# Powers on POOL instead of DVE, one more group of a in seven-product form, tiles due one group sooner

## The reference, cut to what matters

```python
proj = rmsnorm(x) @ w_in                      # v, bg, cg, za, u, zb, ga, gb
ya = (bg * causal_conv3(cg * v)) * silu(za) @ w_out_a
yb = gelu(s5_scan(u, ...))                    # complex diagonal recurrence, 64 groups of 64 states
yb = (yb * sigmoid(yb @ w_glu + b_glu)) * silu(zb) @ w_out_b
x1 = rmsnorm(x + (sigmoid(ga)*ya + sigmoid(gb)*yb) @ w_o)
# second block: modulation by cond @ w_ada, spatial gating, 16 heads of forgetting attention, w_out_2
```

## Time and profile before

| | |
|---|---|
| median of 3 runs | 2487.74 us (2487.32 to 2489.63) |
| the profiled execution, its own time | 2489.72 us |
| its span, first to last instruction | 2488.5 us |
| PE busy | 2465.3 us, 99% |
| DVE busy | 1737.4 us, 70% |
| ACT / POOL busy | 925.6 us / 411.5 us |
| granted PE clock, mean | 0.998 |

### The profile page before, as it was taken

The page is one execution under the profiler, slowest core; times in us unless marked ns, Lnnn a source line. Parts: engine busy times, 40 slices in busy tenths (PEclk is TensorE's granted clock), DMA queues, the critical chain, the costliest instruction groups (busy, mean ns, idle before and its releaser), DMA issues.

```text
span 2488.5 us, 32838 instructions
## 1 busy us (share of the span) xinstructions
PE 2465.3 (99%) x13084; PEld 2170.0 (87%) x13084; DVE 1737.4 (70%) x2313; ACT 925.6 (37%) x1267; POOL 411.5 (17%) x334
## 2 busy tenths in 40 slices
PE   9999999999999999999999999999999999999998
PEld 8888887888888899999888888878888888888888
DVE  7889999998998865666756666567565564467534
ACT  5323222222222245445422223333565564224432
POOL 0035554553543011211000000000000000000001
PEclk9999999999999999999999999999999999999999
DMA  5344444443333288988676777524322222556333
GB/s 203 105 125 145 141 134 129 138 133 110 122 113 109 98 205 200 201 204 182 225 255 217 228 242 231 170 87 152 102 85 77 85 85 86 195 178 210 119 127 127
DMA packets 124888, 378.43 MB, mean 152 GB/s; under 512 B 16192, under 2 KB 19520, under 8 KB 124736
## 3 DMA queue, kind: packets, MB, share of 16 engines
q1 hardware_dynamic: 115520, 342.77, 42.0%
q0 software_dynamic: 9216, 33.56, 7.6%
HBM read 346.84 MB, written 23.07 MB: 149 GB/s over the span
## 4 chain that ended last, share of the span: by engine, by line
PE 48%; DVE 2%; DMA 1%; ACT 0%; issue 0%; DVEq 0%; ACTq 0%; SPq 0%
PE bank L696 13%; PE bank L697 13%; PE bank L698 13%; PE bank L965 2%; PE bank L966 2%; PE bank L964 2%; PE bank L1018 1%; DMA SI<-scr_zb 1%; PE bank L1008 1%; PE bank L928 1%; DVE ACC L1583 0%; PE bank L1001 0%; PE bank L999 0%; DVE WL L1567 0%; PE bank L1060 0%
## 5 line engine op out<-in xcount | busy, mean ns | idle before, releaser
L1567 DVE TENSOR_TENSOR WL<-W,WH 128x1024 fp32r<-128x1024 f32 (+1 forms) x447 | 592.8, 1329 | 385.5 <-ACT WH L1136 384.6
L1136 ACT ACTIVATE WH<-W 128x1024 fp32r<-128x1024 f32 (+1 forms) x447 | 468.8, 1051 | 791.1 <-PE bank L698 475.0
L696 PE MATMUL bank<-hH,WH 128*128 128x512 f32 x1280 | 487.6, 381 | 1.5 <-DVE hL L1861 1.1
L698 PE MATMUL bank<-hH,WL 128*128 128x512 f32 x1280 | 485.9, 380 | 0.0
L697 PE MATMUL bank<-hL,WH 128*128 128x512 f32 x1280 | 485.9, 380 | 0.0
L696 PEld LDWEIGHTS bank<-hH,WH 128*128 128x128 f32 x1280 | 242.5, 189 | 44.9 <-issue 7.3
L698 PEld LDWEIGHTS bank<-hH,WL 128*128 128x128 f32 x1280 | 242.4, 189 | 34.3
L697 PEld LDWEIGHTS bank<-hL,WH 128*128 128x128 f32 x1280 | 242.7, 190 | 33.7
L696 PE MATMUL bank<-h2H,WH 128*128 128x512 f32 x624 | 239.8, 384 | 0.1
L698 PE MATMUL bank<-h2H,WL 128*128 128x512 f32 x624 | 236.6, 379 | 0.0
L697 PE MATMUL bank<-h2L,WH 128*128 128x512 f32 x624 | 236.6, 379 | 0.0
(11 more groups left out here) (365 smaller groups left out, 4898.7 us busy)
## 6 DMA issues: line engine op xcount, KB each, us to landing
W<-in_w SPq DMA_DIRECT2D x292, 512.0 KB, 3.5
W<-in_ada SPq DMA_DIRECT2D x96, 512.0 KB, 4.2
W<-in_w POOLq DMA_DIRECT2D x35, 512.0 KB, 6.0
W<-in_wa SPq DMA_DIRECT2D x32, 512.0 KB, 4.2
W<-in_wo SPq DMA_DIRECT2D x32, 512.0 KB, 3.6
W<-in_wvv SPq DMA_DIRECT2D x32, 512.0 KB, 4.2
WX<-in_w POOLq DMA_DIRECT2D x29, 512.0 KB, 6.3
WX<-in_w SPq DMA_DIRECT2D x24, 512.0 KB, 4.2
```

The lines of the kernel that those rows point to most:

```text
L696: e.matmul(o, wh, xh, start=first, stop=False)
L698: return e.matmul(o, wl, xh, start=False, stop=last)
L1136: e.activation(chunk_parts(n)[0][:, c], raw_chunk(n)[:, c], ACT.Copy).then_inc(sem["hi"], 1)
L1567: e.tensor_tensor(wl[:, c], raw_chunk(n)[:, c], wh[:, c].bitcast(F32), ALU.subtract).then_inc(sem["lo_v"], 1)
```

## The change

Four edits in one:

1. The powers leave DVE. DVE's generator keeps nine empty steps in their place; POOL gets a function `powers()` with the same operations, each waiting for the one before (`prm_p`). POOL calls it as soon as DVE has finished CB (`prm_v`), and before its first `stack_low`.
2. `PARAM_STEPS` is spread: step 10 falls at unit 18 (before: 19), steps 11 and 12 at units 19 and 20, and step 21 at unit 29 (before: 26). The tiles begin at unit 31 (29), take equal shares on all units, and end with group 5 of a (6).
3. `ST_C` goes from 8 to 7: group 7 of a is made as a seven-product pair.
4. The first two projections of wb are woven: pieces 0 to 6 of the first, 0 to 6 of the second, then piece 7 of both.

```diff
-PARAM_STEPS = [min(max(n - 4, 0), 9) + (3 * max(n - 18, 0) + 1) // 2 for n in range(27)]
-TILE_UNIT = 29
-TILE_SHARE = (5, 4)
-SSM_C = 6
-ST_C = 8
+PARAM_STEPS = [min(max(n - 4, 0), 9) + max(n - 17, 0) for n in range(30)]
+TILE_UNIT = 31
+TILE_SHARE = (1, 1)
+SSM_C = 5
+ST_C = 7
...
-        for d, p in enumerate(wb_p):
-            project(p, lambda k: BH[:, k, :], lambda k: BL[:, k, :], b_ready if d == 0 else None, (0,))
+        first = [unit(), None]
+        for i, ks in enumerate((range(7), range(7, 8))):
+            for d in range(2):
+                if (i, d) == (0, 1):
+                    first[1] = unit()
+                n, o = first[d], bank[bank_of[wb_p[d]]][:, :]
+                for k in ks:
...
+                    if d == 0:
+                        b_ready(k)
+                    c = slice(128 * k, 128 * k + 128)
+                    mm = triple(o, WH[:, n % NB, c], WL[:, n % NB, c], pairs(BH[:, k, :]), pairs(BL[:, k, :]),
+                                k == 0, k == 7)
+                if i == 1:
+                    mm.then_inc(sem["used"], 1)
+        for d, p in enumerate(wb_p[2:]):
+            project(p, lambda k: BH[:, k, :], lambda k: BL[:, k, :], None, (0,))
...
-            for big, levels in ((E0, 5), (W0, 4)):
+            for _ in range(9):
+                yield
...
+            def powers():
+                at = [0]
+                def step(ins):
+                    ins.then_inc(sem["prm_p"], 1)
+                    at[0] += 1
+                    e.wait_ge(sem["prm_p"], at[0])
+                e.wait_ge(sem["prm_v"], counts["param"])
+                step(e.tensor_copy(pr, cosz))
+                step(e.tensor_copy(pi, sinz))
+                for big, levels in ((E0, 5), (W0, 4)):
+                    step(e.memset(big[:, 0, :, 0:1], 1.0))
+                    step(e.memset(big[:, 1, :, 0:1], 0.0))
+                    for lv in range(levels):
+                        w = 1 << lv
...
+                        step(e.tensor_tensor(y1, a_r, b_r, ALU.mult))
+                        step(e.tensor_tensor(y2, a_i, b_i, ALU.mult))
+                        step(e.tensor_tensor(o_r, y1, y2, ALU.subtract))
+                        step(e.tensor_tensor(y1, a_r, b_i, ALU.mult))
+                        step(e.tensor_tensor(y2, a_i, b_r, ALU.mult))
+                        step(e.tensor_tensor(o_i, y1, y2, ALU.add))
+                        step(e.tensor_tensor(t1, pr, pr, ALU.mult))
+                        step(e.tensor_tensor(t2, pi, pi, ALU.mult))
+                        step(e.tensor_tensor(nr, pr, pi, ALU.mult))
+                        step(e.tensor_tensor(pr, t1, t2, ALU.subtract))
+                        step(e.tensor_scalar(pi, nr, 2.0, None, ALU.mult))
...
+            powers()
             stack_low(0)
             stack_low(1)
             for _ in range(4):
                 yield
-            e.wait_ge(sem["prm_v"], counts["param"])
             e.wait_ge(*nth("xl", 31))
             table(0, 0)
             table(0, 1)
```

More of the change, by code:

```diff
@@ L58 @@
     "sums": 1, "rms_v": 1, "rms_a": 1, "spread": 1, "rsa": 1, "u_rd": 1,
-    "prm": 16, "prm_v": 1, "cb0": 1, "ssm_v": 14, "ssm_p": 6, "ssm_a": 2, "ssm_lu": 1, "ssm_lb": 1,
+    "prm": 16, "prm_v": 1, "prm_p": 1, "cb0": 1, "ssm_v": 14, "ssm_p": 6, "ssm_a": 2, "ssm_lu": 1, "ssm_lb": 1,
     "ssm_bu": 1, "ssm_out": 1, "skip": 1,
@@ L458, in ssm_phases @@
         if n < TILE_UNIT:
-            return min(PARAM_PHASES, PARAM_STEPS[min(n, 26)])
+            return min(PARAM_PHASES, PARAM_STEPS[min(n, 29)])
         return PARAM_PHASES + 130 * tile_share(n) // tile_share(tiles_to)
@@ L898, in b_ready @@
             e.wait_ge(*nth("g_v", k))
-        for d, p in enumerate(wb_p):
-            project(p, lambda k: BH[:, k, :], lambda k: BL[:, k, :], b_ready if d == 0 else None, (0,))
+        first = [unit(), None]
[5 more added lines that the diff above has]
+                for k in ks:
+                    if k == 0:
+                        for w in bank_free[wb_p[d]]:
+                            e.wait_ge(*w)
+                    if d == 0:
[7 more added lines that the diff above has]
+            project(p, lambda k: BH[:, k, :], lambda k: BL[:, k, :], None, (0,))
         def a_ready(k):
@@ L2547, in stack_low @@
                 e.tensor_tensor(ul, URAW[0:32, j % 2, :], ul.bitcast(F32), ALU.subtract).then_inc(sem["ssm_lu"], 1)
+            def powers():
[4 more added lines that the diff above has]
+                    e.wait_ge(sem["prm_p"], at[0])
+                sinz, cosz, t1, t2 = (sm(i) for i in range(18, 22))
+                pr, pi, nr = (sm(i) for i in range(27, 30))
+                tmp, tmp2 = (T[:, i, :].rearrange("p (j n) -> p j n", n=16) for i in (2, 3))
+                e.wait_ge(sem["prm_v"], counts["param"])
[6 more added lines that the diff above has]
+                        w = 1 << lv
+                        a_r, a_i = big[:, 0, :, 0:w], big[:, 1, :, 0:w]
+                        o_r, o_i = big[:, 0, :, w:2 * w], big[:, 1, :, w:2 * w]
+                        b_r = pr.unsqueeze(2).to_broadcast([128, 32, w])
+                        b_i = pi.unsqueeze(2).to_broadcast([128, 32, w])
+                        y1, y2 = tmp[:, :, 0:w], tmp2[:, :, 0:w]
+                        step(e.tensor_tensor(y1, a_r, b_r, ALU.mult))
[9 more added lines that the diff above has]
+                        step(e.tensor_scalar(pi, nr, 2.0, None, ALU.mult))
             def table(j, part):
```

## The result

| | before | after |
|---|---|---|
| median, both measured in the same rounds | 2488.68 us | 2507.36 us |
| profiled execution's span | 2488.5 us | 2507.4 us |
| ratio after / before | | 1.0078, 95% interval 1.0064 to 1.0092 |

The change makes the kernel 18.7 us slower. The forecast was 2502.7 us, its range 2484 to 2516: 14 us over this median of the kernel before, 15 us over the one shown ahead of the prediction.

What follows compares the result with a forecast made beforehand. PE, busy for 99% of the span, was taken as the bound, with DVE setting the pace beside the rows. 2489.7 - 17.0 + 16.0 + 16 = 2504.7, less 2.0 to the median: 2502.7 us, range 2484 to 2516.

Steps and rivals of the forecast that it cites:

- The stand at `drive(0)`: PE at unit 29 waits for POOL's chain of powers and first low stack: 14.3 us plus slow clock, 16.0 us lost.
- Rival 3: POOL much later, each operation at its 1.79 ratio to DVE: 28.9 us lost before the first drive, 2515.6 us; chance 0.1.
- the tiles' start: Tile 0 starts some 20 us later than before, with its tables ready by then: costs nothing.
- Denser tiles beside a: One tile in 3.48 units overloads DVE beside a: 1.2 us a tile, 16 us lost, bounds nothing and 29 us.
- Readout waits gone beside the rows: Three PE waits at readouts, two from rounding, go as readouts fall two units behind DVE: 5.8 + 1.7 = 7.5 us gained.
- Unit 26: PE's wait for a weight split queued behind the powers on DVE goes with its slow clock: 2.9 + 1.7 = 4.6 us gained.
- Group 7: Seven products instead of a plain group of a: PE takes 38.00 instead of 41.45 us, 3.4 us gained.
- The weave: PE's wait for the last `BL` before the eighth piece of the first wb unit goes: 1.5 us gained.
- The Trainium skill's lock: Two-SBUF-input DVE operations and SBUF-reading POOL operations lock each other out: nine splits each hold POOL's chain about 1.0 us.

## Why the prediction was right, point by point

On the profiled executions the change cost 19.1 us where the forecast had 15.0; 2.8 of these 4.1 us are in the first term.

**The stand at `drive(0)`**: right in its mechanism and near in size, 16.0 forecast, 18.8 measured. The start was put at 118.4 us (118.89), the length at 55 us (56.5), the stand at 14.3 us (15.9). The fixed part of 0.18 us and the 2.1 ns a column, from POOL's long operations, hold at 32 columns: 0.25 us forecast, 0.24 to 0.27 measured. Of the 2.8 us that it was short, 1.6 lie in the stand itself and 1.2 in the clock after it: 1.7 us from a spell of 3.4 us, 2.9 measured. The granted clock was 0.50 already from 166 us on, during the stand, and stayed there 5.8 us past it. Rival 3, the fixed ratio of POOL to DVE, fell: without the 8.5 us of locks the chain took 48 us, and the powers took DVE 33 us, as the prediction reads it: a ratio of 1.45. The Trainium skill's 1.96 ("GPSIMD Engine Reference", section "3.1 Elementwise — side-by-side cycle accounting") is a ratio for a long sum and doesn't carry over to small operations: a 128 x 32 product took POOL 0.24 us and DVE 0.19. Shown by the run with the powers on DVE: 18.0 us.

**What it said of the tiles' start** ("the tables are ready by then: nothing") was right only because PE stood. The run with the low stacks in the middle showed 12 us of DVE's waiting in that place. That the forecast didn't need this term is luck: a reader who had repaired the stand by it would have been disappointed by more than half.

**Denser tiles beside a**: forecast 16 between bounds of 0 and 29, measured 15.5 and 0.9 at the entry. That DVE is over its capacity was argued from rows, but the 1.2 us a tile were picked between the bounds and not worked out; that they hit so closely is luck. Shown by three runs: gone with the old pace and with seven and six shares, less with short taps. It is a load of DVE, not arrears: starting the tiles 16 us earlier, or with 12 us of arrears, left these waits as they were. Where I put them was half right: the largest came before drives and splits, the last readout cost nothing to speak of.

**Readout waits gone beside the rows**: forecast 7.5, measured 7.1. One cause, rounding of the shares against the units, was shown from the other side: with shares of five and four they came back at the two readouts that rounding moved. The wait at the first readout was not rounding but arrears of DVE, as the prediction has it: without the stand, with the powers on DVE, 1.0 us of it is there again.

**Unit 26**: 4.6 forecast, and gone. **Group 7**: 3.4 forecast, 3.4 in the windows. **The weave**: the 1.5 us did go, but the step that gave them to the weave was wrong; without it they are gone too, with the powers on DVE. The Trainium skill's lock ("SBUF — State Buffer", section "SBUF: two separate sides") carried two terms, the nine prolonged operations of the chain and DVE's cost beside a; the trace bears it out, a 0.25 us product of POOL takes 1.27 us beside a split.

## What to carry to other kernels

Before work goes to an engine that seems free, ask who waits for what stands behind it in that engine's queue, and price the whole dependent chain, wait for wait: 105 operations of 0.15 to 1.7 us with 0.08 us between took 56.5 us, whatever the engine's busy share. Here spreading the work over more units on its old engine did what the move was to do. When side work is laid on a grid of units by a formula, look at the rounding at each point where one engine waits for another, and at the load of the fuller engine in each stage, not on the mean.

## What the runs showed of the hardware that I had not expected

The spell of half clock (1.2 instead of 2.4 GHz) is not always 3.4 us: after the stand of 15.9 us it went on for 5.8 us past the restart, and after the wait of 3.7 us at 759.6 us it lasted 6.8 us in all, where the wait of 3.4 us before the third readout in the kernel before had brought 3.4 us. Nor does the length of the wait decide it. The same wait of 3.7 us beside a brought 3.4 us with the powers on DVE and with the stacks in the middle. And in the run with the weave alone a wait of 3.4 us before the third readout brought none at all; its 16 matmuls took 1.92 us, where those of the earlier trace rows took 3.43:

```profile
397.78 1.92 PE L768 MATMUL bank<-HH,CB 128*32 128x512 f32 x16 [3.21 <-issue]
```

So the 1.7 us that the prediction adds to a wait of this size was 0, 1.7 or 3.1 us here, and runs that differ by 2 or 3 us can differ in this alone.

Beside POOL's table work a tap of the convolution on DVE took 1.0 us more on the mean than alone, with 32 columns as with 512. Fewer columns saved what they take alone, and nothing of the wait.
